# Holding one gate tile back for the last stage, and spreading its turnings among the weight chunks

## The reference

```python
h = rms_norm(x, norm_w[i])
proj = h @ w_in[i]                       # 2048 x 16592
(g_qkv, g_z, g_b, g_a, r_feat, r_z, s_u, s_z, gate_logits) = _split_cols(proj, SPLIT_SIZES)
o_a = gdn_branch(g_qkv, g_z, g_b, g_a, ...)
o_b = rwkv7_branch(r_feat, r_z, ...)
o_c = s5_branch(s_u, s_z, ...)           # ends: y = gelu(y); y * sigmoid(y @ glu_w + glu_b) * silu(z)
branches = jnp.stack([o_a, o_b, o_c], axis=2)
branch_proj = jnp.einsum('blnc,ncd->blnd', branches, w_branch[i])     # three of 1024 x 2048
gates = jax.nn.sigmoid(gate_logits.reshape(bsz, seq, N_BRANCH, D_MODEL) + gate_b[i])
merged = jnp.sum(gates * branch_proj, axis=2)
x = x + merged @ w_out[i]                # and a last rms_norm
```

## Time and profile before

| | |
|---|---|
| timed runs | 2308.97 us median of 3 (2306.59 to 2311.85) |
| profiled execution, its own time | 2303.7 us |
| its span | 2301.9 us |
| TensorE busy | 2186.2 us, 95% |
| VectorE, ScalarE busy | 1554.0 us (68%), 1069.1 us (46%) |
| mean granted TensorE clock | 0.990 of full speed |
| waits of TensorE in the RWKV stage | on the load of rwk_be 1.5; on rwk_QT 1.3 in 2; on rwk_inv_x 0.4; "issue" 1.3 and 0.2 |
| eviction to mm_stage | 672 ns for each of two |
| mm_hi, mm_lo of 128x1024 | about 1.05 and 1.22 us |
| turned copies: hi, lo | 0.58 us; two lo in 1.29 us |
| addition of a gate's bias (L3212) | 1.22 us |
| load of b's rows (ob, 1 MB) | 5.4 us from issue to landing |

### The profile page before, as it was taken

One profiled execution on the slowest core, in us unless ns is written; L12 is line 12 of the kernel. 1 busy time (PEld: TensorE's weight loads), 2 busy tenths in 40 slices (PEclk: granted clock), 3 DMA queues, 4 the chain that ended last, 5 costly groups with the idle time before them and its releaser, 6 DMA issues.

```text
span 2301.9 us, 35226 instructions
## 1 busy us (share of the span) xinstructions
PE 2186.2 (95%) x14268; PEld 1793.8 (78%) x14268; DVE 1554.0 (68%) x2302; ACT 1069.1 (46%) x1488; POOL 115.4 (5%) x188
## 2 busy tenths in 40 slices
PE   7999989999999999999999989998999999989997
PEld 6889668888788789887777767776677777768886
DVE  5665475557997455667999686665875566667754
ACT  5444466445444656554343563333454333345443
POOL 0000001001001001000000100001010000011000
PEclk9999999999999999999999999999999999999999
DMA  7666337757778557857665753349687344487753
GB/s 235 189 191 189 94 108 265 286 189 233 265 277 294 183 172 238 332 181 279 215 223 171 256 165 122 127 130 348 207 307 268 124 123 135 142 296 253 247 185 120
DMA packets 222482, 481.15 MB, mean 209 GB/s; under 512 B 14896, under 2 KB 51552, under 8 KB 217584
## 3 DMA queue, kind: packets, MB, share of 16 engines
q1 hardware_dynamic: 200112, 372.91, 49.2%
q0 software_dynamic: 22208, 105.99, 12.5%
HBM read 421.45 MB, written 57.40 MB: 208 GB/s over the span
## 4 chain that ended last, share of the span: by engine, by line
PE 68%; DVE 19%; DMA 5%; ACT 4%; issue 3%; POOL 0%; ACTq 0%; DVEq 0%; SPq 0%; POOLq 0%
PE mm_acc L308 38%; PE mm_acc L312 19%; DVE mm_lo L213 6%; DMA mm_raw<-in_w_in 2%; ACT mm_hi L206 1%; DVE gdn_cv L1882 1%; DVE s_q L2983 1%; DVE s_p L2968 1%; DVE s_r L2976 1%; DVE s_p L2969 1%; DVE s_r L2978 1%; PE in_turn L412 1%; PE rwk_bank L2418 1%; PE even_lg_ps L1027 1%; PE rwk_bank L1451 1%
## 5 line engine op out<-in xcount | busy, mean ns | idle before, releaser
L213 DVE TENSOR_TENSOR mm_lo<-mm_raw,mm_hi 128x1024 fp32r<-128x1024 f32 (+4 forms) x672 | 789.9, 1184 | 483.6 <-ACT mm_hi L206 473.7
L206 ACT CAST mm_hi<-mm_raw 128x1024 fp32r<-128x1024 f32 (+4 forms) x672 | 680.8, 1019 | 748.5 <-PE mm_acc L312 715.2
L308 PE MATMUL mm_acc<-mm_hi,mm_aT_hi 128*128 128x512 f32 (+5 forms) x2208 | 860.2, 390 | 23.1 <-ACT mm_hi L206 18.1
L308 PE MATMUL mm_acc<-mm_hi,mm_aT_lo 128*128 128x512 f32 (+5 forms) x2208 | 853.1, 387 | 0.0
L312 PE MATMUL mm_acc<-mm_lo,mm_aT_hi 128*128 128x512 f32 (+5 forms) x2208 | 597.3, 388 | 13.9 <-DVE mm_lo L213 13.8
L308 PEld LDWEIGHTS mm_acc<-mm_hi,mm_aT_hi 128*128 128x128 f32 x2208 | 418.0, 189 | 102.3 <-ACT mm_hi L206 19.1
L312 PEld LDWEIGHTS mm_acc<-mm_lo,mm_aT_hi 128*128 128x128 f32 x2208 | 408.1, 189 | 92.7 <-DVE mm_lo L213 21.2
L308 PEld LDWEIGHTS mm_acc<-mm_hi,mm_aT_lo 128*128 128x128 f32 x2208 | 418.1, 189 | 72.6 <-issue 4.3
L308 PE MATMUL mm_acc<-mm_hi,in_yT_hi 128*128 128x512 f32 x256 | 100.9, 394 | 0.2 <-ACT mm_hi L206 0.2
L258 ACT ACTIVATE mm_stage<-mm_acc,mm_row_scale 128x512 f32<-128x512 f32 (+3 forms) x104 | 64.4, 672 | 76.7 <-PE mm_acc L312 76.7
L308 PE MATMUL mm_acc<-mm_hi,in_yT_lo 128*128 128x512 f32 x256 | 99.7, 390 | 0.0
(11 more groups left out here) (634 smaller groups left out, 2059.1 us busy)
## 6 DMA issues: line engine op xcount, KB each, us to landing
mm_raw<-in_w_in SPq DMA_DIRECT2D x384, 512.0 KB, 5.1
mm_raw<-in_w_out SPq DMA_DIRECT2D x96, 512.0 KB, 5.5
mm_raw<-in_w_in SPq DMA_DIRECT2D x72, 464.0 KB, 4.2
mm_raw<-in_w_branch SPq DMA_DIRECT2D x48, 512.0 KB, 5.5
proj<-mm_stage SPq DMA_DIRECT2D x46, 512.0 KB, 3.1
mm_raw<-in_w_in SPq DMA_DIRECT2D x32, 416.0 KB, 4.8
home_tab<-s5t_tab POOLq DMA_DIRECT2D x4, 2048.0 KB, 9.5
s_tab<-home_tab POOLq DMA_DIRECT2D x8, 1024.0 KB, 5.9
```

Source lines behind the costliest of these rows:

```text
L206: self.nc.scalar.copy(self.hi[:, c % RING, :, 0:t.w], self.raw[:, c % RAW, :, 0:t.w]).then_inc(self.hi_done, 1)
L213: self.nc.vector.tensor_tensor(self.lo[:, c % RING, :, 0:t.w], self.raw[:, c % RAW, :, 0:t.w], self.hi[:, c % RING, :, 0:t.w].bitcast(F32) ...
L308: last = nc.tensor.matmul(self.acc[s][m][:, 0:t.w], t.aT[a][:, k0 + k, m * P:(m + 1) * P], self.hi[:, c % RING, k, 0:t.w], start=(k0 + k = ...
```

## The change

- `late` is added in two parts, of which the first, `narrow`, has (N_IN - O_SZ) % TN columns. `late` is then both together.
- The RWKV stage fills with `late[5:-1]`, 8 tiles (64 chunks) in place of 9 (72). The last tile is given to `tail` as `held`, and is multiplied there first, behind `ph.enter`.
- The turning of a, b and c is done one group at a time with a chunk behind each (`turn_among`, `copies_among`): a's among the last four chunks of the held tile, b's among the four chunks of a's first `w_branch` tile, c's among those of b's.
- The branches are multiplied in the order a, b, c in place of a, c, b, and the gates loaded accordingly. POOL waits before the last gate's load until the held tile is stored.
- ScalarE's silu of `z`, the first sigmoid, and VectorE's `gate_rows(0)` and `gate(0)` come behind the held tile's chunks and a's copies.

```diff
-                mm.sp(sp, 2 * n_glu + len(order) * n_br + n_last)
+                mm.sp(sp, n_held + 2 * n_glu + len(order) * n_br + n_last)
...
+                def turn_among(i):
+                    for job in plan[i]:
+                        turner.turn(pe, [job])
+                        mm.pe(pe, 1)
+                    turned(i)
+
                 ph.enter(pe)
+                mm.pe(pe, 2)
+                pe.wait_ge(y_in, 16)
+                row_turner.turn(pe, jobs_r[0:2])
+                mm.pe(pe, n_held - 6)
+                turn_among(0)
                 for i in range(2):
                     pe.wait_ge(y_lo, i + 1)
                     mm.pe(pe, 2)
-                pe.wait_ge(y_in, 16)
-                row_turner.turn(pe, jobs_r[0:2])
-                turn(0)
-                mm.pe(pe, 2)
                 row_turner.turn(pe, jobs_r[2:4])
-                mm.pe(pe, 2 * n_glu - 6)
-                turned(0)
-                mm.pe(pe, n_br)
-                turn(1)
-                turn(2)
-                turned(1)
-                mm.pe(pe, n_br)
-                turned(2)
-                mm.pe(pe, n_br)
+                mm.pe(pe, 2 * n_glu - 4)
+                turn_among(1)
+                turn_among(2)
                 mm.pe(pe, n_br)
...
+                def copies_among(i):
+                    for j, job in enumerate(plan[i]):
+                        turner.copy_hi(act, [job], base[i] + j)
+                        mm.act(act, 1)
...
-                mm.act(act, 2)
+                mm.act(act, n_held - 4)
+                copies_among(0)
                 act.wait_ge(z_in, 32)
                 nc.scalar.activation(z[:, :, :], z[:, :, :], ACT.Silu).then_inc(silu, 1)
-                mm.act(act, n_glu - 2)
-                copies(0)
                 sigmoid(0)
-                mm.act(act, n_glu + n_br)
-                copies(1)
-                copies(2)
-                mm.act(act, 2 * n_br)
+                mm.act(act, 2 * n_glu)
+                copies_among(1)
+                copies_among(2)
+                mm.act(act, n_br)
...
+                def copies_among(i, after=lambda: None):
+                    for j, job in enumerate(plan[i]):
+                        turner.copy_lo(dve, [job], base[i] + j)
+                        mm.dve(dve, 1)
+                        if j == 1:
+                            after()
...
-                mm.dve(dve, n_glu)
+                mm.dve(dve, n_held - 4)
+                copies_among(0)
                 dve.wait_ge(silu, 1)
...
                 gate_rows(0)
-                copies(0)
                 gate(0)
-                mm.dve(dve, 2)
+                mm.dve(dve, 4)
                 gate_rows(1)
-                mm.dve(dve, n_glu)
-                dve.wait_ge(sig, 2)
-                zrows = z[:, :, :].rearrange("p m (h c) -> p h m c", h=2)
-                TT(zrows, zrows, yrows, ALU.mult).then_inc(oc_done, 1)
-                gate(1)
-                mm.dve(dve, n_br - 2)
-                copies(1)
-                copies(2)
-                product(1)
+                mm.dve(dve, 2 * n_glu - 4)
+
+                def combine():
+                    dve.wait_ge(sig, 2)
+                    zrows = z[:, :, :].rearrange("p m (h c) -> p h m c", h=2)
+                    TT(zrows, zrows, yrows, ALU.mult).then_inc(oc_done, 1)
+                    gate(1)
+
+                copies_among(1, combine)
+                copies_among(2, lambda: between(1))
                 product(2)
...
+            narrow = (N_IN - O_SZ) % TN
+            for_s5, for_gdn, for_rwkv, narrow, late = (mm.add(p2["w_in"], home, c) for home, c in (
+                (None, (O_SU, O_SZ)), (proj, (0, c_rwkv)), (proj, (c_rwkv, O_SU)), (proj, (O_SZ, O_SZ + narrow)), (proj, (O_SZ + narrow, N_IN))))
+            late = narrow + late
...
-                    rwkv(nc, "rwk", a, mm, for_gdn + for_rwkv, late[5:], proj, *rw, carry, rp["lnx_w"], rp["lnx_b"], ob, rows.load)
-                    tail(nc, "tail", mm, rows, glu, branch, out2, proj, oa, ob, p2["s5_glu_b"], p2["gate_b"], x3, a["final_norm_w_2"], out[0])
+                    rwkv(nc, "rwk", a, mm, for_gdn + for_rwkv, late[5:-1], proj, *rw, carry, rp["lnx_w"], rp["lnx_b"], ob, rows.load)
+                    tail(nc, "tail", mm, rows, late[-1:], glu, branch, out2, proj, oa, ob, p2["s5_glu_b"], p2["gate_b"], x3, a["final_norm_w_2"], out[0])
```

More of the change, by code:

```diff
@@ L3000, in load, with tail @@
         pool.dma_start(self.yt[:, :, :], self.yg.rearrange("(k p) t -> p k t", p=P)).then_inc(self.y_in, 16)
-def tail(nc, name, mm, early, glu, branch, last, proj, oa, ob, glu_b, gate_b, x, norm, out):
+def tail(nc, name, mm, early, held, glu, branch, last, proj, oa, ob, glu_b, gate_b, x, norm, out):
     K, NBR = S_W, 3
     KT, TILES = K // P, D // TN
-    ORDER = (0, 2, 1)
     SLOTS = 3
@@ L3047, in tail @@
         jobs_m = [operand(mg[:, n % 2, :, :], 4 * n, 4, mm.aT, (folded, 2 * (n + 1))) for n in range(TILES)]
-        plan = [jobs_a, jobs_c, jobs_b] + jobs_m
+        plan = [jobs_a, jobs_b, jobs_c] + jobs_m
         base = [sum(len(j) for j in plan[:i]) for i in range(len(plan) + 1)]
@@ L3052, in tail @@
         for n in range(TILES):
-            for i, b in enumerate(ORDER):
-                branch[n * NBR + i].aT = bT[b]
+            for b in range(NBR):
+                branch[n * NBR + b].aT = bT[b]
         for t in last:
             t.rows, t.rows_in = xt, (res_in, 16)
-        n_glu, n_br, n_last = ticks(glu[:1]), ticks(branch[:1]), ticks(last)
+        n_held, n_glu, n_br, n_last = ticks(held), ticks(glu[:1]), ticks(branch[:1]), ticks(last)
         order = [(n, i) for n in range(TILES) for i in range(NBR)]
@@ L3077, in gates @@
                     n, j = order[i]
-                    c0 = ORDER[j] * D + n * TN
+                    c0 = j * D + n * TN
                     pool.dma_start(gt[:, i % SLOTS, :, :], rowsv(proj)[:, :, O_GL + c0:O_GL + c0 + TN]).then_inc(gate_in[i % SLOTS], 16)
-                    pool.dma_start(gbt[:, i % SLOTS, :], bcast_rows(gate_b[ORDER[j], n * TN:(n + 1) * TN])).then_inc(gate_in[i % SLOTS], 16)
+                    pool.dma_start(gbt[:, i % SLOTS, :], bcast_rows(gate_b[j, n * TN:(n + 1) * TN])).then_inc(gate_in[i % SLOTS], 16)
                 pool.dma_start(ab[:, :, :], rowsv(oa)).then_inc(a_in, 16)
@@ L3094, in _ @@
                     pool.wait_ge(*free(branch[i - SLOTS]))
+                    if i == len(order) - 1:
+                        mm.wait_stored(pool, held)
                     gates(i)
@@ L3229, in branch_out @@
                     if j == 0:
-                        dve.wait_ge(turner.turned, base[n + 2] if n >= 2 else base[3])
+                        dve.wait_ge(turner.turned, base[n + 2] if n >= 2 else base[2])
                     if j and 2 * n + j > 1:
@@ L3354, in program @@
             c_rwkv = -(-O_RF // TN) * TN
-            for_s5, for_gdn, for_rwkv, late = (mm.add(p2["w_in"], home, c) for home, c in (
-                (None, (O_SU, O_SZ)), (proj, (0, c_rwkv)), (proj, (c_rwkv, O_SU)), (proj, (O_SZ, N_IN))))
+            narrow = (N_IN - O_SZ) % TN
+            for_s5, for_gdn, for_rwkv, narrow, late = (mm.add(p2["w_in"], home, c) for home, c in (
+                (None, (O_SU, O_SZ)), (proj, (0, c_rwkv)), (proj, (c_rwkv, O_SU)), (proj, (O_SZ, O_SZ + narrow)), (proj, (O_SZ + narrow, N_IN))))
+            late = narrow + late
             glu = mm.add(p2["s5_glu_w"], None)
-            branch = [t for n in range(D // TN) for b in (0, 2, 1) for t in mm.add(p2["w_branch"][b], None, (n * TN, (n + 1) * TN))]
+            branch = [t for n in range(D // TN) for b in range(3) for t in mm.add(p2["w_branch"][b], None, (n * TN, (n + 1) * TN))]
             out2 = mm.add(p2["w_out"], None)
```

## The result

The changed kernel takes 2313.61 us by the median of 20 runs (2309.62 to 2323.11), the kernel before 2306.23 in its 20 (2302.88 to 2311.85): a ratio of 1.0035 [1.0026, 1.0043]. It is 7.4 us slower; the forecast was 2306.8, or 2.2 us faster. That 2313.6 still lies in the stated range (2299.5 to 2314.5) is in part luck: the range stood on a median of three runs, 2.7 us above that of twenty. The profiled execution took 2310.1 (span 2308.3), 6.4 more than before.

What follows compares the result with a forecast made beforehand. TensorE was 95% busy, so only its idle and low-clock time could be won or lost. Losses summed to 15.5 us against 17.7 in the last stage now: -2.2, so 2306.8 us by the median, range 2299.5 to 2314.5.

Steps and rivals of the forecast that it cites:

- The rounds of heads: Four rounds in the RWKV stage: thinner filler uncovers waits on QT, Hs and the inverse, 2.4 us lost (0 to 16).
- The RWKV stage's start: Before the first turning: 1.8 us more wait for rwk_be with less filler, plus 1.1 us of low clock behind it.
- The last stage: From its entry to the end: shorter entry wait and spread turnings against new waits, forecast as -7.5 us together.
- The entry: Start of the last stage: entered 13.8 us after the RWKV stage's last products, TensorE waiting 3.6 us.
- The copies' waits at the turnings: Last stage: with a chunk behind each turning group, the waits of 5.0 and 4.1 us go.
- ScalarE's unspread chain: Between held tile and GLU: its chain makes TensorE wait 2.5 us for the third GLU chunk, plus 0.8 for clock.
- drain: Behind ScalarE's table load: the skill's extra 1.4 us or so, left out; with it the wait would be 3.9 us.
- The clock: Low clock behind idle gaps: 1.5 us added behind the 3.6 us entry wait, less behind shorter waits.
- Narrow tile, order of branches, POOL and SP: The empty narrow tile, the new branch order and the POOL and SP changes: each priced at 0.
- Rival 2: RWKV stage held up by its filler: rounds lose 9.6 us in place of 2.4, total 2314.0; chance 0.17.
- Rivals 1 and 3: 1: rounds lose nothing, clock stays, 2301.0, chance 0.25. 3: table switch up to 3.9 us longer, 2310.7, chance 0.11.

Runs made afterwards that it cites:

- e11: The changed kernel with TensorE's already met wait for vv ahead of the rounds of heads written 128 more times; ratio to before 1.0058.
- e13: The kernel before with 192 further already met waits on TensorE ahead of the rounds of heads; ratio to before 1.0067.
- e16: The changed kernel with 384 further already met waits on TensorE ahead of the rounds of heads; ratio to before 1.0107.
- e9: The kernel before with 64 further already met waits on TensorE ahead of the rounds of heads; ratio to before 0.9999.
- e5: The kernel before with 32 useless one-column matmuls where TensorE enters the RWKV stage; ratio to before 1.0063.
- e14: The kernel before with 320 further already met waits on TensorE ahead of the rounds of heads; ratio to before 1.0096.
- e3: The changed kernel, but the preparation fills with 4 tiles in place of 5 and the RWKV stage keeps its nine; ratio to before 1.0018.
- e15: The changed kernel with 256 further already met waits on TensorE ahead of the rounds of heads; ratio to before 1.0070.
- e6: The changed kernel with 32 useless one-column matmuls where TensorE enters the RWKV stage; ratio to before 1.0054.
- e8: The changed kernel with the held tile's first two chunks multiplied before the wait for the last stage's gate; ratio to before 1.0018.
- e10: The changed kernel with 64 further already met waits on TensorE ahead of the rounds of heads; ratio to before 1.0036.
- e1: The kernel before with only the last filler tile moved from the RWKV stage to the last stage's head; ratio to before 1.0053.
- e12: e7 with exactly 7 filler steps at each point of the RWKV stage and 15 at its last three; median 2303.4 us.
- e2: The changed kernel with all nine filler tiles left in the RWKV stage, a's turnings among the last four GLU chunks; ratio to before 1.0002.
- e7: e2 with a's turnings moved earlier, among GLU chunks 3 to 6; median 2299.72 us, ratio to before 0.9974.
- e4: The changed kernel with its RWKV filler weighted so that the rounds of heads keep their old amount and other points less; ratio to before 1.0085.

## Why the prediction was wrong

**The rounds of heads (2.4 forecast, 12.0 found) are the step that failed.** I asked at each wait on VectorE or ScalarE how much room it had, and for that it was a fair size: those waits rose by 2.5 us. By luck in part, for the rise came from inv_x more than from the waits that I had priced, on QT and Hs. What I left out was TensorE's own supply of instructions ("issue" 1.5 to 5.8, of which 4.8 at block edges) and the half clock behind a stall, which there wasn't any of before (up to 5.0 of the 5.1 us of slower work). The rows had it: "issue" stood in the list of waits in the front table, and I priced it at nothing.

How much of it is the thinner filler? With the low clock at the head of the rounds taken off in e11 (1.7 us) and e13 to e16, six kernels with the whole filler lost 0, 1.0, 2.2, 2.8, 4.0 and 5.3 us (before, e9, e13, e5, e14, e3), mean 2.6; eight with the thin one 7.3 to 16.9 (e15, e6, e16, e8, after, e10, e11, e1), mean 11.6. e12, with 4.0 us out, lost 4.3. I take the difference, some 9 us, as the filler's, and some 3 as luck of place that the kernel before had. Of 16 us of filler taken out, then, about 7 come back. This is an estimate from one profile of each kernel. Counting after, e1 and e8, whose RWKV program is the same, as one, and e2 and e7 with before, it is 8.4. Pairs with the same shift lie 5 (e5, e6) to 13 us (e9, e10) apart. e4 is outside this: whole filler in the rounds, 17.1 lost. Its outer points were thinner, its edges elsewhere; which of the two did it stays open. Why profiles of the same RWKV program (after, e1, e8) range from 10.9 to 16.9 is open too, beyond what e1's slow execution explains.

**The RWKV stage's start (1.8 and 1.1 forecast, 2.6 found)** has the size but not the place. There was no wait on rwk_be; TensorE came later, slowed by a low clock ahead of the stage, and waited 1.4 for rwk_src instead. Behind that wait the clock stayed whole up to the rounds, where I had added 1.1. e10 shows 1.0 on rwk_be, e1 1.5.

```profile
1689.20:1695.90 6.70, 6.70 (x22) 5.73 (x23) 6.67 (x7) 2.27 (x3) 1.02 (x2) 0.50 0.27 78
```

**The last stage (-7.5 forecast, -6.2 found)** was right by its waits, 7.0 us against 7.2. The entry came 13.8 us after the products as predicted: 1998.3, where TensorE's products end, to 2012.12, where ScalarE starts the split, with two mm_lo on VectorE in between in place of three. The copies' waits at the turnings went. ScalarE's unspread chain made the third GLU chunk late by 2.61. No drain stands behind the table load: the load of 1.28 began at 2037.61 and silu at 2038.90. The Trainium skill ("ScalarE: Activation LUTs", section "What ACT_TABLE_LOAD costs") adds one of about 1.4; here the row decides against it, and the wait came as by the load alone. The chunk behind that wait took 4.4 us instead of 2.72: its half clock cost 1.7, where I had put 0.8.

**The clock** behind the 3.5 us wait: 0.91 in the entry's window against 0.83, with a matmul at 0.63 us from the sixth on in place of 0.39. The whole chunk cost 1.7 us extra, against 1.5 forecast. The prediction says that its two rows contradict the 3 us that it cites both ways; only the 1.85 us does, 2.98 is under 3.

```profile
2008.80:2014.30 5.50, 2.00 (x7) 1.67 (x8) 3.21 (x3) 3.45 (x5) 2.36 (x4) 0.91 0.72 245
```

**Narrow tile, order of branches, POOL and SP** showed no wait of their own, as forecast; none was tried alone.

**The rivals.** Rival 2 named the place and the price: 9.6 in the rounds, 2314.0 against 2313.6 measured. Its reason, a chain of points in which every exposed wait shifts the rest, is only the smaller part: waits on other engines gave 2.5 of 12.0. Its total is in part luck too: the rounds lost 12.0, not 9.6. Rivals 1 and 3 fall: low clock followed the waits, and the table load took its row's time. My chances gave rival 2 0.17 because I counted the waits that the profile could name.

The change's parts were thus worth, in its profile: the tile's removal from the RWKV stage +14.6 us in its start and its rounds, everything in the last stage together -6.2. e7 gains in the last stage (4 us in its profile, 6 by the ratio) and leaves the rounds alone.

## What to carry to other kernels

Filler in a stage of small matmuls covers more than the waits that the profile ties to an engine. TensorE works on each filler matmul for 0.23 us and on one of 16 columns for 0.011 (64 in 0.72), so filler makes a block of 256 instructions last longer while the next one comes. With stalls of at most 0.7 us named "issue", in the kernel before, the clock also stayed whole. Before taking any out, look at what the stage loses to "issue", and count the filler as returned only in part (here 7 of 16 us by estimate). Price a move at both ends separately, and try each end alone: the end that was meant to gain did, and it could be had without the other. A change of TensorE's program also moves every later block edge, so a difference of 2 to 5 us in such a stage may be place and nothing else.

## What the runs showed of the hardware

TensorE's program comes in blocks of 256 instructions, 16384 bytes each, and here no two followed each other in less than 3.3 us. Where a run of small matmuls used a block up sooner, TensorE stood still for up to 3.4 us (e10), until 1.1 to 1.6 us after the next had moved.

Waits whose condition is already met are not free in numbers: 128, 192, 256, 320 and 384 of them put 3.3, 6.8, 10.4, 13.8 and 17.4 us before the next matmul, 3.5 us for each further 64, or 55 ns each. 64 showed none: their 32 instructions passed while TensorE was busy with matmuls issued before them (e9, 1753.2 to 1756.7).

Matmuls of one column are dear: 32 of them, recorded as 64, took 11.57 us, 0.18 each, and half clock set in while they ran.

```profile
1722.55 11.57 PE L2401 MATMUL rwk_bank<-mm_ident 128*128 128x1 f32 x64
```

```profile
1725.20:1738.70 13.50, 13.50 (x58) 12.72 (x59) 0.00 (x0) 0.59 (x1) 0.00 (x0) 0.51 0.71 289
```
